# Softmax attentions with keys as rows and queries as columns, two heads at a time in the array

## The reference

```python
s = (q @ k.T).astype(float32) * scale          # mask or bias added
p = softmax(s)                                  # over the keys (and the sink)
o = p @ v
o_diff = (softmax(s1) - lam * softmax(s2)) @ v  # differential heads
```

## Time and profile before

| | |
|---|---|
| median of three runs | 4078.21 us (4074.97 to 4082.68) |
| profiled execution, its own time | 4074.97 us |
| its span, first to last instruction | 4073.1 us |
| TensorE busy / weight loads | 3628.8 us (89%) / 2828.1 us (69%) |
| VectorE / ScalarE / POOL busy | 1905.3 (47%) / 1247.6 (31%) / 1054.3 us (26%) |
| mean granted TensorE clock | 0.923 of 2.4 GHz |

### The profile page before, as it was taken

The page is one execution under the profiler, slowest core; times in us unless marked ns, Lnnn a source line. Parts: engine busy times, 40 slices in busy tenths (PEclk is TensorE's granted clock), DMA queues, the critical chain, the costliest instruction groups (busy, mean ns, idle before and its releaser), DMA issues. The chain is left out here.

```text
span 4073.1 us, 46528 instructions
## 1 busy us (share of the span) xinstructions
PE 3628.8 (89%) x17568; PEld 2828.1 (69%) x17568; DVE 1905.3 (47%) x3523; ACT 1247.6 (31%) x1778; POOL 1054.3 (26%) x599
## 2 busy tenths in 40 slices
PE   2989899999967779999998977899999998869998
PEld 2865578878656758886575545788899466557887
DVE  7342242437354457473607684654345507752111
ACT  2225532223321132223004543322244104443222
POOL 2300344444424333433000002344400000014444
PEclk9976999999978979999997978999999998879999
DMA  6410134432200014442110001244345220002221
GB/s 227 173 65 1 42 137 147 186 119 93 82 1 1 1 52 165 144 168 102 52 63 11 1 1 42 98 155 174 142 164 175 74 73 1 1 22 89 90 97 64
DMA packets 54942, 355.62 MB, mean 87 GB/s; under 512 B 5888, under 2 KB 6912, under 8 KB 19456
## 3 DMA queue, kind: packets, MB, share of 16 engines
q1 hardware_dynamic: 54496, 351.35, 23.8%
q10 hardware_dynamic: 288, 2.10, 0.1%
HBM read 351.32 MB, written 2.10 MB: 87 GB/s over the span
## 5 line engine op out<-in xcount | busy, mean ns | idle before, releaser
L376 POOL TENSOR_TENSOR W_LO<-ring,W_HI 128x2048 fp32r<-128x2048 f32 (+1 forms) x181 | 747.5, 4130 | 2251.0 <-ACT W_HI L364 2251.0
L432 PE MATMUL PS<-H_HI,W_HI 128*128 128x512 f32 (+1 forms) x1888 | 713.4, 378 | 33.2 <-DVE H_LO L775 26.3
L434 PE MATMUL PS<-H_HI,W_LO 128*128 128x512 f32 (+1 forms) x1888 | 703.4, 373 | 0.0
L433 PE MATMUL PS<-H_LO,W_HI 128*128 128x512 f32 (+1 forms) x1888 | 703.2, 372 | 0.0
L364 ACT ACTIVATE W_HI<-ring 128x2048 fp32r<-128x2048 f32 (+1 forms) x218 | 373.8, 1715 | 476.3 <-PE PS L422 476.0
L432 PEld LDWEIGHTS PS<-H_HI,W_HI 128*128 128x128 f32 x1888 | 359.9, 191 | 98.9 <-issue 37.6
L434 PEld LDWEIGHTS PS<-H_HI,W_LO 128*128 128x128 f32 x1888 | 359.2, 190 | 63.2
L433 PEld LDWEIGHTS PS<-H_LO,W_HI 128*128 128x128 f32 x1888 | 360.0, 191 | 59.5 <-issue 0.2
L817 DVE SCALAR_TENSOR_TENSOR PS<-ring,SC,PS 128x256 f32<-128x256 f32 x792 | 388.0, 490 | 27.8
L420 PE MATMUL PS<-HID_HI,W_HI 128*128 128x512 f32 (+1 forms) x880 | 325.4, 370 | 4.9 <-DVE W_LO L376 4.0
L422 PE MATMUL PS<-HID_HI,W_LO 128*128 128x512 f32 (+1 forms) x880 | 323.8, 368 | 0.0
(11 more groups left out here) (278 smaller groups left out, 5522.8 us busy)
## 6 DMA issues: line engine op xcount, KB each, us to landing
ring<-w_tiles SPq DMA_DIRECT2D x273, 1024.0 KB, 4.8
ring<-d_tiles SPq DMA_DIRECT2D x80, 704.0 KB, 4.1
X<-xT SPq DMA_DIRECT2D x1, 2048.0 KB, 19.1
WORK<-rope_tables ACTq DMA_DIRECT2D x2, 1024.0 KB, 7.0
outT<-H SPq DMA_DIRECT2D x8, 256.0 KB, 2.2
CN<-consts SPq DMA_DIRECT2D x1, 1377.0 KB, 14.2
X<-ctxT SPq DMA_DIRECT2D x1, 1024.0 KB, 21.4
PR<-params SPq DMA_DIRECT2D x1, 465.5 KB, 3.5
```

The costliest lines, as they stand in the source:

```text
L376: eng.tensor_tensor(W_LO[:, b, 0:w], ring[:, g % SLOTS, 0:w], W_HI[:, b, 0:w].bitcast(F32), ALU.subtract).then_inc(sig("tile_split"), 1)
L432: pe.matmul(to, hi[:, cols(k, j)], x_hi(k), start=k == 0, stop=False)
L433: pe.matmul(to, hi[:, cols(k, j)], x_lo(k), start=False, stop=False)
L434: mm = pe.matmul(to, lo[:, cols(k, j)], x_hi(k), start=False, stop=k == n - 1)
```

## The change

Jobs become tasks. A task is a pair of heads ("units") whose queries and keys lie in different rows of the array (partitions 0-63 and 64-127; for two-map heads 32 of each half) and whose outputs go to different columns (PSUM partitions 0-63 and 64-127); a two-map pair gives two tasks, the second added with factor minus lambda. Layer 0 has 4 tasks, layer 3 has 8, layer 2 has 8 and 8 small ones for the context queries; layers 2 and 3 have one call of the attention functions in place of two.

A task first makes scores queries by keys, for the maxima alone (`q_steps`, one PSUM bank per unit), which VectorE reduces; TensorE transposes the four columns of maxima, and VectorE spreads them into `MAX_ROWS`. Then it makes the scores again, keys by queries (`steps`, one per tile of 128 keys, up to 512 queries), and an fp32r matmul adds minus the maximum of each query in PSUM. ScalarE takes the exponential of that; POOL zeroes the masked triangles, or VectorE adds a bias ahead of it, for which `pe_bias_turned` transposes `BT` into `BT_TURNED`. The result needs no transpose: TensorE multiplies by V and, with ones, makes the sums, repeated on 64 partitions. ScalarE turns the sums into reciprocals by Ln and Exp, VectorE multiplies. `attention_order` writes one order for all queues, with maxima up to two tasks ahead. The queries of window and neighbourhood heads are scaled by 0.125 where they are copied out of PSUM. The old functions and `mixer_jobs`' lists go out whole and are not repeated.

```diff
-        S_SB = ...; PT = ...
-        def pe_attention(pe, jobs): ...      # with dve_attention, act_attention
+        WEIGHT_BUFS = 6
+        def attention_order(tasks):
+            ...
+            def may_come(p):
+                kind, q, _ = q_items[at]
+                return q <= p + 2 and (kind == "maxima" or q <= p + 1)
+            ...
+            for g in range(len(steps) + 2):
+                p = steps[g][0] if g < len(steps) else len(tasks)
+                if g < len(steps):
+                    while ("rows", p, 0) in q_items[at:]:
+                        order.append(q_items[at])
+                        at += 1
+                    order.append(("scores", p, steps[g][1]))
+                    order += next_maxima(p)
+                    at += len(next_maxima(p))
+                if closing is not None:
+                    order.append(("heads", closing, 0))
+                    closing = None
+                if g >= 2:
+                    q, x = steps[g - 2]
+                    order.append(("outputs", q, x))
+                    if x == len(tasks[q]["steps"]) - 1:
+                        closing = q
+                if g < len(steps):
+                    order += next_maxima(p)
+                    at += len(next_maxima(p))
+            return order + [("heads", closing, 0)]
...
+        def pe_attention(pe, tasks):
+            def maxima(p, j):
+                wait_maxima_bank(("maxima", p, j))
+                for i, k0, k1, o in tasks[p]["q_steps"][j]["products"]:
+                    for u, unit in enumerate(tasks[p]["units"]):
+                        a = maxima_bank(u) + o
+                        mm = pe.matmul(PS[:, a:a + k1 - k0], unit["q"][:, i * P:(i + 1) * P], unit["k"][:, k0:k1],
+                                       start=True, stop=True)
+                mm.then_inc(sig("maxima_scored"), 1)
...
+            def scores(p, x):
+                ...
+                for n, (c, q0, q1, o) in enumerate(s["parts"]):
+                    for u, unit in enumerate(task["units"]):
+                        a = score_bank(g, u) + o
+                        if c is not None:
+                            pe.matmul(PS[:, a:a + q1 - q0], unit["k"][:, c * P:(c + 1) * P], unit["q"][:, q0:q1],
+                                      start=True, stop=False)
+                    for u, unit in enumerate(task["units"]):
+                        ...
+                        mm = pe.matmul(PS[:, a:a + q1 - q0], MINUS[r, :], MAX_ROWS[r, p % 2, q0:q1], start=c is None, stop=True)
...
+            def outputs(p, x):
+                ...
+                if x == 0:
+                    before = p if task["own_banks"] is None else p - task["own_banks"]
+                    if before:
+                        pe.wait_ge(sig("heads_done"), b_h + before)
+                ...
+                    if c is not None:
+                        for u, unit in enumerate(task["units"]):
+                            f = unit["off"]
+                            pe.matmul(PS[f:f + 64, task["n_at"] + q0:task["n_at"] + q1], unit["v"](c),
+                                      weight_tile(tasks, g, u)[:, o:o + q1 - q0], start=first, stop=end, skip_group_check=True)
+                    for u, unit in enumerate(task["units"]):
+                        ...
+                        mm = pe.matmul(PS[f:f + 64, task["t_at"] + q0:task["t_at"] + q1], ones[k, 0:64],
+                                       weight_tile(tasks, g, u)[k, o:o + q1 - q0], ...)
...
+        def dve_attention(dve, tasks, chain):
+            def maxima(p, j): ...
+                        if mask is None:
+                            ins = dve.tensor_reduce(to, src.rearrange("p (t c) -> p t c", t=tiles), AX_X, ALU.max)
+                        else:
+                            ins = dve.tensor_tensor_reduce(out=MASKED[u][:, 0:w], in0=src, in1=mask(u), scale=1.0, scalar=NEG,
+                                                           op0=ALU.add, op1=ALU.max, accum_out=to)
+            def rows(p): ...
+                dve.tensor_tensor(MAX_ROWS[:, p % 2, 0:nq * P].rearrange("p (a x) -> p a x", a=nq), src, own,
+                                  ALU.mult).then_inc(sig("maxima_read"), 1)
+            def scores(p, x): ...            # steps with a bias alone
+                    dve.tensor_tensor(weight_tile(tasks, g, u), PS[:, score_bank(g, u):score_bank(g, u) + T], s["bias"](u),
+                                      ALU.add).then_inc(sig("scores_biased"), 1)
+            def heads(p): ...
+                    if task["minus"] is None:
+                        ins = dve.tensor_tensor(to, n, scale, ALU.mult)
...
+        def act_attention(act, tasks, chain):
+            def scores(p, x): ...
+                        act.activation(tile[:, lo:hi], src, ACT.Exp, scale=task["scale"]).then_inc(sig("exps_ready"), 1)
+            def outputs(p, x): ...           # after a task's last step
+                chain(act.activation(SCALES[:, 0:w], PS[:, task["t_at"]:task["t_at"] + w], ACT.Ln))
+                act.activation(SCALES[:, 0:w], SCALES[:, 0:w], ACT.Exp, scale=-1.0).then_inc(sig("scales_ready"), 1)
+            act.preload_act_table_set("natural_log_exp_and_others")
+            act.activation(MINUS[:, :], const("negones"), ACT.Copy).then_inc(sig("minus_ready"), 1)
...
+        def pool_attention(pool, tasks): ... # affine_select of 128 x 128 after the exponential, signal weights_masked
...
+        def pe_bias_turned(pe):
+            pe.wait_ge(sig("bias_masked"), base("pe", "bias_masked", 1) + 1)
+            for h in range(4):
+                for j in range(7):
+                    o = h * 1024 + j * P
+                    mm = pe.transpose(PS[:, o:o + P], BT[:, h, 12 - 2 * j:14 - 2 * j, :].rearrange("p s c -> p (s c)"), ident)
+                mm.then_inc(sig("bias_turned"), 1)
+        def act_bias_turned(act): ...        # four copies of 128 x 896 to BT_TURNED
...
-                    act_copy_tiles(act, f"in{layer}", Q2, segs, 2, 2, chunks, nb=2)
+                    act_copy_tiles(act, f"in{layer}", Q2, segs, 1, 2, chunks, nb=2, scale=0.125)
+                    act_copy_tiles(act, f"in{layer}", Q2, segs, 1, 3, chunks, nb=2)
...
                     pe_bias(pe, layer - 2)
+                    pe_bias_turned(pe)
                     ph.end(pe)
-                    singles, doubles = mixer_jobs(layer)
-                    pe_attention(pe, singles)
-                    ph.end(pe)
-                    pe_attention(pe, doubles)
+                    pe_attention(pe, mixer_tasks(layer))
```

More of the change, by code:

```diff
@@ new lines, in attention_table @@
+        def attention_table(tasks):
+            step, q_item, biased, masked = {}, {}, {}, {}
+            for kind, p, x in attention_order(tasks):
+                if kind in ("maxima", "rows"):
+                    q_item[kind, p, x] = len(q_item)
+            for p, task in enumerate(tasks):
+                for x in range(len(task["steps"])):
+                    step[p, x] = len(step)
+                    if task["steps"][x]["bias"] is not None:
+                        biased[p, x] = len(biased)
+                    if task["steps"][x]["masks"]:
+                        masked[p, x] = len(masked)
+            return step, q_item, biased, masked, list(step)
@@ new lines, in pool_attention @@
+        def pool_attention(pool, tasks):
+            step, q_item, biased, masked, steps = attention_table(tasks)
+            b_e = base("pool", "exps_ready", 2 * len(step))
+            for p, x in masked:
+                g = step[p, x]
+                for u in range(2):
+                    pool.wait_ge(sig("exps_ready"), b_e + 2 * g + u + 1)
+                    for o, way in tasks[p]["steps"][x]["masks"]:
+                        v = weight_tile(tasks, g, u)[:, o:o + P]
+                        ins = pool.affine_select(out=v, in_=v, compare_op=ALU.is_ge, fill=0.0, base=0,
+                                                 pattern=[[way, P]], channel_multiplier=-way)
+                    ins.then_inc(sig("weights_masked"), 1)
@@ new lines, in unit, with plain_step, context_steps, main_task @@
+        def unit(q, k, rows, off, v, sink=None):
+            return dict(q=q, k=k, rows=rows, off=off, v=v, sink=sink)
+        def plain_step(c, q0, q1, masks=(), bias=None):
+            return dict(parts=[(c, q0, q1, q0)], masks=masks, bias=bias)
+        def context_steps():
+            return [dict(products=[(i, T, TA, 0), (i + 1, T, TA, TC)], reads=[(0, 2, TC, 1, i, None)]) for i in (0, 2)]
+        def main_task(units, scale, q_steps, steps, out, kinds=2, minus=None, weights_at=None):
+            return dict(units=units, scale=scale, q_steps=q_steps, steps=steps, out=out, kinds=kinds, minus=minus, tiles=NT,
+                        own_banks=None, n_at=3072, t_at=3584, weights_at=weights_at)
@@ new lines, in context_task @@
+        def context_task(units, scale, out, n, minus=None):
+            parts = [(4, 0, TC, 0), (5, 0, TC, TC)]
```

(21 more changed lines are left out.)

491 lines of the change are left out of this document (258 added, 233 removed).

## The result

| | median, us | lowest to highest |
|---|---|---|
| before | 4074.99 | 4032.99 to 4082.68 (20 runs) |
| after | 4089.86 | 4081.44 to 4096.63 (20 runs) |

The ratio is 1.0043, with a 95% interval of 1.0028 to 1.0058: the changed kernel is slower by 0.4%, more than the measurement is uncertain. 4040 with a gain had been forecast. The profiled execution took 4086.85 us, its span is 4085.0 (before: 4074.97 and 4073.1).

A forecast was written before the change was run, and what follows sets the result against it. TensorE bounds causal and single-map attentions, VectorE the two-map ones. Causal -37.2, layer 3 +2.4, layer 2 -0.8, turned bias +14.6, sub-norm -7.8, stick-breaking -8 sum to -36.8 us: forecast 4040 us, range 3960 to 4160.

The forecast's parts named there:

- the clock in layers 2 and 3: TensorE in both layers' attentions: full clock assumed, except 3.9 us extra per layer at the start for clock 0.50.
- predicted sum: Attention plus sub-norm of a layer, from streaming, shape changes, waits, start and end: 311.1 us layer 2, 253.0 layer 3.
- The rival of the clock: Causal stays at 1.2 GHz (+28 us) and two-map tasks run at clock 0.74 (+63): 4131 us, chance 0.14.
- Waits: TensorE waiting for maxima reads and the heads' product: 20 us causal, 35 layer 3, 55 layer 2, 110 together.
- (b): Next task's first outputs wait for the heads' product, queued on VectorE behind a maxima item: 2.4 to 3.2 us, context 2.0.
- Pairs: Two heads' matmuls in different rows or columns of TensorE's array cost what one costs; all streaming then takes 411 us.
- The rivals on the pairs: TensorE pairs overlap in part (4143 us, 0.07), column pairs run one after the other (4234, 0.09), or none overlap (4450, 0.05).
- Causal: Layer 0's causal attention: four tasks of 16.0 us plus 10.3, 74.3 against 111.5 us, -37.2, at clock 1.0 after the start.
- Stick-breaking: Stick-breaking stage loses two table loads per head, its loop going from 10.3 to about 9.3 us: -8 us.
- turned bias: 28 transposes at the slow clock and a last copy of 0.9 us: +7.3 us in each of two layers, +14.6.
- Sub-norm: Sub-norm after the attention loses four table loads of 1.28 us, the first beside matmuls: -3.9 us per layer, -7.8.
- The add-and-maximum reading: VectorE's combined add and maximum over scores: 0.69 us at 512 columns, or 1.38 if two runs, +45 us in all.

The follow-up runs named there:

- fill_all: Changed kernel plus two filler matmuls ahead of each wait for the heads and one behind each maxima item before a stage's first scores, all three attentions: 4042.94 us.
- heads_first: Changed kernel with the product of the heads issued on VectorE before the maxima item of its step, no longer behind it: 4029.95 us.
- loads_only: Kernel before, plus only a request for the exponential-and-logarithm table set ahead of its causal and single-map attentions: 4059.74 us.

## Why the prediction was wrong

The sum said -36.8; the spans differ by +11.9, 48.7 off. By its steps:

- **Failed: the clock in layers 2 and 3.** The prediction put "3.9 on top for the clock of 0.50 that the bias stage leaves" and otherwise counted every column at full clock, because "the single-map stages reach 0.93". Measured are 105.4 and 44.4 us at 1.2 GHz, of which TensorE works for 87.0 and 34.1; half of that, 43.5 and 17.0 us, is lost, where 3.9 each was counted. Layer 2 came out 35.8 over its predicted sum and layer 3 13.8. Holding the clock by fillers, all else left in place, takes 34.6 and 12.7 of them back. It has two parts: the start (37.5 us low in layer 2, 23.9 in layer 3, where six maxima items alternate with VectorE's reads; the prediction summed the reads as idle time and did not ask what they do to the clock), and spells behind the waits for the heads. The rival of the clock, held at 0.14, had the right sign and, at 4131, too high a price. It named a wait per task beside the 32 rows of the two-map tasks, and put a part of the loss in causal. Causal gained; the loss lies behind the waits, and at the start, where the items are of window heads with 64 rows.
- **Waits: there, and somewhat over-priced.** (b) sums to about 37 us in layer 2 and 21 in layer 3; TensorE waited 28.3 and 14.0 for the heads, 1.9 and 2.0 at a time (the wait shown, of a two-map task, is 2.83). That fill_all meets the predicted sums so closely hides this in part, for its fillers, 2 x 0.88 us, stand in these waits and fill the shorter ones out. A second wait was hardly counted: for the reading of a task's last maxima, ahead of their transpose (L1072), TensorE stands 9.9 us in layer 2 and 6.7 in layer 3, and the prediction has 1.6 per stage "for the rows" and 0.1 per transpose. So the sum of the waits is near the measured one partly because one is too high and one too low, which is luck. What the prediction missed is that a wait costs the clock behind it too: of the 41 us that heads_first took from layer 2, 18 are idle time and 23 clock.
- **Pairs: right.** A step repeats after 3.16 us against 3.17. The Trainium skill ("TensorE: Matmul & The Clock Gate", Part 3, "Measured speedup vs the span model") has concurrent tiles lose a fifth of the ideal; this trace, with two tiles and not three or four, shows no loss for pairs of rows and of columns. The rivals on the pairs fall.
- **Causal: -41.9 for -37.2**, right in kind. Its clock rose to 0.86, from 0.50, where over 0.9 had been the sign. The waits were over-priced: TensorE waited three times 1.7 us for the heads, where 4 x 2.9 was counted.
- **Stick-breaking -8.8 for -8, turned bias +16.0 for +14.6: right.** loads_only shows the first by itself. In the second the transposes took 5.5 and 4.8 us, less than the 6.4 counted; a wait of 2.8 us for `MINUS` (L1263), which ScalarE writes behind its copies and a table load of 1.28 us, was not counted.
- **Sub-norm: half.** From the attention's last matmul to the next stage's first it is 2.2 and 1.8 us shorter, not 3.9 each. The loads did go; but this stretch now has the last heads' product and reciprocals in it, which the prediction counted in the attention. In loads_only, where that is not so, it is 3.9 and 4.5.

The add-and-maximum reading, bounded between 0.69 and 1.38 us at 512, took the lower: VectorE in layer 2 by form,

```profile
L1161 DVE CUSTOM_DVE_ANT_0 BIG<-PS,WORK 128x512 f32<-128x512 f32 x16 | 10.4, 688 | 16.4 <-PE PS L1064 16.4
```

What the loss per us at the low clock means: for each us in which TensorE works it is 0.5, as the table under heads_first shows. The Trainium skill ("TensorE: Matmul & The Clock Gate", Part 1, "HAM oscillation — how this bites in real kernels") reckons the cost of throttled time so, and this trace agrees for its working part. By the whole low time, as the comparisons with fillers give it, it is 0.28 to 0.38, because part of such a spell is idle anyway and the fillers are partly longer than the waits they stand in. In layer 2 fill_all takes 40.3 us of clock away and its fillers are about 5.7 us longer than the idle time that they replace: 34.6 of the stage.

## What to carry to other kernels

Price a new wait on TensorE with the clock behind it: here the idle time that heads_first removed from an otherwise dense stage had cost 0.5 times (layer 3) and 1.2 times (layer 2) its own length again. Look at what the awaited instruction stands behind on its queue: moving one product ahead of one reduction brought 60 us, as much as the new attention in layer 0 did together with the table request, which alone was worth 17. Where a wait can't go, a matmul without use in its place is cheap, and it is also the experiment that tells the cost of the clock from that of the wait.

## What the runs showed of the hardware that was not expected

The clock fell to 1.2 GHz behind waits of only 1.6 to 2.8 us, with full work on both sides of them, as a wait of 1.64 us in heads_first shows, whose outputs then take 1.97 us; the Trainium skill ("TensorE: Matmul & The Clock Gate", Part 1, "A second HAM failure mode: psum-queue depth-cycling") tells of short idle times between groups of matmuls that make the clock swing, and this trace agrees. Not every wait does it: in the changed kernel's layer 3 four of the six waits for the heads of 1.6 to 2.8 us were followed by such a spell and two (1.99 and 1.64 us) were not, and none of the three of 1.6 to 1.9 us in causal was. What decides is not shown.

The rows of that wait in heads_first:

```profile
3437.46 1.97 PE L1118 MATMUL PS<-BIG 128*64 128x512 f32 x4 [1.64 <-DVE H L1206]
```

At the start of layer 2's attention items of 1.2 to 2.1 us of matmuls alternate with idle times of about 1, and it stayed low for 37.5 us; with fillers of 512 columns in them all of the attention had 6.4 (fill_all). And the same code can come out with a different share of low clock when what is ahead of it moves: the old attention of layer 3 had 79.4, 80.0, 95.0 and 98.3 us low in four kernels, and took 235.6, 236.3, 241.2 and 240.1 us.
